# An expert loop over eight experts, with each expert's scatter in two parts and the body's last unit in two transfers

## What is computed

```python
g_idx = argmax(xt @ w_group + b_group)              # one of 4 groups of experts
top_v, top_i = lax.top_k(e_in, 2)                   # two of the 4 experts in that group
top_w = softmax(top_v) * g_w
expert = g_idx * 4 + top_i                          # 16 experts in all
y = (silu(xb @ w_gate[e]) * (xb @ w_up[e])) @ w_down[e]     # for the tokens xb of expert e
out = segment_sum(y * w, token)                     # back to the tokens, weighted
x = x + out
```

## Time and profile before

| | |
|---|---|
| median of 3 runs | 1190.21 us (1189.8 to 1192.86) |
| the profiled execution | 1189.95 us |
| its span, first to last instruction | 1188.2 us |
| mean granted TensorE clock | 0.996 of full speed |
| TensorE busy | 1133.9 us (95% of the span) |
| VectorE, ScalarE, GpSimd busy | 431.2, 174.7, 8.1 us |
| DMA | 439.30 MB, mean 370 GB/s |
| expert loops on TensorE | about 170 to 597 us, and 757 to 1184 us |

### The profile page before, as it was taken

How to read it: one execution, slowest core, us unless ns; L and a number is a source line. 1 busy time by engine, 2 the same in 40 slices (tenths; PEclk the granted TensorE clock), 3 DMA queues, 4 the chain that set the end, 5 groups by cost and what they waited for, 6 DMA issues and landing times.

```text
span 1188.2 us, 13852 instructions
## 1 busy us (share of the span) xinstructions
PE 1133.9 (95%) x5646; PEld 524.0 (44%) x5646; DVE 431.2 (36%) x766; ACT 174.7 (15%) x344; POOL 8.1 (1%) x36
## 2 busy tenths in 40 slices
PE   6998999999999999999889999999999999999997
PEld 5985443333333333333379764433333333333332
DVE  4655144232222332232276671532222323322222
ACT  3426110000000000000054261100000100000000
POOL 2000000000000000000000000000000000000000
PEclk9999999999999999999989999999999999999999
DMA  9677269999999999999994373899999999999996
GB/s 359 167 306 320 105 245 429 429 426 429 427 429 428 429 427 429 427 430 427 416 367 185 143 285 140 350 429 426 429 428 427 429 427 430 426 430 426 430 426 266
DMA packets 53904, 439.30 MB, mean 370 GB/s; under 512 B 14192, under 2 KB 14192, under 8 KB 29296
## 3 DMA queue, kind: packets, MB, share of 16 engines
q1 hardware_dynamic: 53872, 438.85, 89.1%
HBM read 437.79 MB, written 1.05 MB: 369 GB/s over the span
## 4 chain that ended last, share of the span: by engine, by line
PE 85%; DMA 9%; DVE 3%; ACT 2%; issue 1%; SPq 1%; another core or an unknown queue 0%; ACTq 0%; DVEq 0%
PE bank L1561 49%; PE bank L1471 8%; PE bank L1498 5%; PE bank L1573 5%; PE bank L1540 4%; DMA ring<-in_moe_w_gate 4%; DMA ring<-in_moe_w_up 4%; PE bank L1464 4%; PE bank L1605 1%; PE bank L1549 1%; PE bank L1355 1%; PE bank L1266 1%; PE bank L1412 1%; PE bank L1598 1%; PE bank L1306 1%
## 5 line engine op out<-in xcount | busy, mean ns | idle before, releaser
L1561 PE MATMUL bank<-ring,work 128*64 128x512 f32 x2304 | 510.8, 594 | 11.1 <-DVE work L1237 6.3
L1561 PEld LDWEIGHTS bank<-ring,work 128*64 128x64 f32 x2304 | 161.6, 137 | 343.3 <-issue 327.0
L1227 DVE TENSOR_SCALAR work<-work 128x512 f32<-128x512 f32 x32 | 13.7, 427 | 456.2 <-ACT work L786 456.2
L1229 DVE RECIPROCAL work<-work 128x512 f32<-128x512 f32 x32 | 107.3, 3353 | 1.1
L789 ACT ACTIVATE attention<-bank 128x512 f32<-128x512 f32 x32 | 19.1, 597 | 531.2 <-PE bank L1561 531.2
L1540 PE MATMUL bank<-x_sb,root_y 128*64 128x512 f32 x272 | 64.2, 593 | 2.2 <-DVE root_y L1115 2.2
L1234 DVE TENSOR_TENSOR work<-bank,work 128x512 f32<-128x512 f32 x32 | 22.1, 692 | 113.0 <-PE bank L1561 113.0
L1561 PE MATMUL bank<-ring_over_qk,work 128*64 128x512 f32 x256 | 57.7, 593 | 2.5 <-DMA ring_over_qk<-in_moe_w_gate 2.5
L1561 PE MATMUL bank<-ring_over_v,work 128*64 128x512 f32 x256 | 57.6, 592 | 0.0
L1561 PE MATMUL bank<-ring_spare,work 128*64 128x512 f32 x256 | 57.6, 592 | 0.0
L1498 PE MATMUL bank<-ring,hn 128*128 128x512 f32 x128 | 55.7, 593 | 1.2 <-ACT hn L705 0.7
(11 more groups left out here) (227 smaller groups left out, 939.6 us busy)
## 6 DMA issues: line engine op xcount, KB each, us to landing
ring<-in_moe_w_gate SPq DMA_DIRECT2D x48, 2048.0 KB, 26.9
ring<-in_moe_w_up SPq DMA_DIRECT2D x48, 2048.0 KB, 29.0
ring<-in_moe_w_down SPq DMA_DIRECT2D x48, 2048.0 KB, 27.6
ring_over_qk<-in_moe_w_gate SPq DMA_DIRECT2D x16, 2048.0 KB, 30.2
ring_over_v<-in_moe_w_up SPq DMA_DIRECT2D x16, 2048.0 KB, 30.0
ring_spare<-in_moe_w_down SPq DMA_DIRECT2D x16, 2048.0 KB, 30.7
ring<-in_ab_w_in SPq DMA_DIRECT2D x12, 1024.0 KB, 14.1
ring<-in_c_w_in SPq DMA_DIRECT2D x12, 1024.0 KB, 14.5
```

What stands on the lines that cost most here:

```text
L1229: nc.vector.reciprocal(sig, sig).then_inc(s.gate_step, 1)
L1561: last = mm(b[SLOTS * half:SLOTS * (half + 1), :], left(h, k), expert_rhs(slot, k, half), start=(h == 0 and k == 0), stop=(h == 1 and k == ...
```

## The change

Three things change, all in the expert loop.

First, a body is eight experts (an octet) instead of four: it runs twice in each layer in place of four times, and SyncE runs one pass and has one written out. Second, the scatter of the expert in front is done in two parts: its first two products (the first 128 tokens) stand between the two up units, the other two where all four stood. Third, the last unit of each body, in slot 11, is loaded by two transfers of 1024 KB; the second has a semaphore of its own, `last_rows`, and TensorE waits for it in the middle of that unit.

```diff
-QUAD = 4
-LAPS = (12, 12)
+OCTET = 8
+LAPS = (12, 12, 12, 12)
...
+SPLIT_SLOT, SPLIT_USE = PLACES[-1]
...
-            def load_unit(layer, slot, u, e):
+            def load_unit(layer, slot, u, e, split_unit=False):
                 w = (moe_w_gate, moe_w_up, moe_w_down)[u // 2][layer]
                 src = w[bass.ds(e, 1)].rearrange("e (h p s) n -> (e h) p (s n)", h=2, s=SUB)[u % 2]
+                if split_unit:
+                    sp.dma_start(ring[slot][:, 0:UNIT // 2], src[:, 0:UNIT // 2]
+                                 ).then_inc(layers[layer].unit_loaded[slot], 16)
+                    sp.dma_start(ring[slot][:, UNIT // 2:], src[:, UNIT // 2:]
+                                 ).then_inc(layers[layer].last_rows, 16)
+                    return
                 sp.dma_start(ring[slot][:, :], src).then_inc(layers[layer].unit_loaded[slot], 16)
...
-                    load_unit(layer, slot, i % UNITS, N_EXPERTS - QUAD + i // UNITS)
+                    load_unit(layer, slot, i % UNITS, N_EXPERTS - OCTET + i // UNITS,
+                              i == OCTET_UNITS - 1)
...
+                def one_half(b, left, octet, turn, h, u):
+
+                    slot, lap = place(turn, u)
+                    pe.wait_ge(s.unit_loaded[slot], octet * (USES[slot] * 16)
+                               + ((WIN if slot < UNITS else 0) + 16 * (lap + 1)))
+                    for k in range(SUB):
+                        if (turn, u) == (OCTET - 1, UNITS - 1) and k == SUB // 2:
+                            pe.wait_ge(s.last_rows, octet * 16 + 16)
+                        for half in range(2):
+                            last = mm(b[SLOTS * half:SLOTS * (half + 1), :], left(h, k),
+                                      expert_rhs(slot, k, half), start=(h == 0 and k == 0),
+                                      stop=(h == 1 and k == SUB - 1))
+                    last.then_inc(s.unit_used[slot], 1)
...
-                def scatter(count, k):
+                def scatter(count, k, tiles):
 
                     pe.wait_ge(s.giveT_ready, count)
                     pe.wait_ge(s.y_out, count)
-                    for t in range(NT):
+                    for t in tiles:
...
-                        two_halves(UP, tokens, quad, k, (2, 3))
+                        one_half(UP, tokens, octet, k, 0, 2)
+                        if k >= 1:
+                            scatter(turns(octet, k), k - 1, (0,))
+                        one_half(UP, tokens, octet, k, 1, 3)
...
                         if k >= 1:
-                            scatter(turns(quad, k), k - 1)
+                            scatter(turns(octet, k), k - 1, (1,))
...
-                    scatter(turns(quad, QUAD), QUAD - 1)
+                    scatter(turns(octet, OCTET), OCTET - 1, range(NT))
```

More of the change, by code:

```diff
@@ L142, in __init__ @@
         self.unit_loaded = [sem(f"unit_loaded{u}") for u in range(RING + 1)]
+        self.last_rows = sem("last_rows")
         self.unit_used = [sem(f"unit_used{u}") for u in range(RING + 1)]
@@ L514, in _ @@
                 sp.wait_ge(slots_ready, layer + 1)
[L515 to L522, removed]
+                last_octet = sp.value_load(last_octets[0:1, layer:layer + 1],
+                                          min_val=N_EXPERTS // OCTET - 1,
+                                          max_val=ROUNDS * N_EXPERTS // OCTET - 1)
+                with sp.Fori(0, last_octet) as octet:
+                    first = (octet & (N_EXPERTS // OCTET - 1)) * OCTET
+                    next_first = ((octet + 1) & (N_EXPERTS // OCTET - 1)) * OCTET
+                    for i in [*range(RING + 1, OCTET_UNITS), *range(RING + 1)]:
                         slot, lap = PLACES[i]
@@ L778, in _ @@
                 act.wait_ge(slots_ready, layer + 1)
[L779 to L785, removed]
+                last_octet = act.value_load(last_octets[0:1, layer:layer + 1],
+                                          min_val=N_EXPERTS // OCTET - 1,
+                                          max_val=ROUNDS * N_EXPERTS // OCTET - 1)
+                with act.Fori(0, last_octet + 1) as octet:
+                    for k in range(OCTET):
+                        now, after = turns(octet, k + 1), turns(octet, k + 2)
+                        act.wait_ge(*used(s, octet, k, 1))
                         act.activation(sig, GATE[:, :], ACT.Exp, scale=-1.0).then_inc(s.gate_exp, 1)
                         leave_gathered(after)
-                        act.wait_ge(*used(s, quad, k, 5))
+                        act.wait_ge(*used(s, octet, k, 5))
                         act.activation(y, Y[:, :], ACT.Copy).then_inc(s.y_out, 1)
                 for q in (2, 3):
-                    act.wait_ge(s.scattered, scattered_all(last_quad, q))
+                    act.wait_ge(s.scattered, scattered_all(last_octet, q))
                     if layer + 1 == LAYERS:
@@ L1218, in _ @@
                 dve.wait_ge(slots_ready, layer + 1)
[L1219 to L1226, removed]
+                last_octet = dve.value_load(last_octets[0:1, layer:layer + 1],
+                                          min_val=N_EXPERTS // OCTET - 1,
+                                          max_val=ROUNDS * N_EXPERTS // OCTET - 1)
@@ L1227, in _ @@
+                with dve.Fori(0, last_octet + 1) as octet:
+                    for k in range(OCTET):
+                        make_take(layer, turns(octet, k + 1))
+                        dve.wait_ge(s.gate_exp, turns(octet, k + 1))
                         ts(sig, sig, 1.0, None, ALU.add).then_inc(s.gate_step, 1)
-                        dve.wait_ge(s.gate_step, quad * (2 * QUAD) + (2 * k + 1))
+                        dve.wait_ge(s.gate_step, octet * (2 * OCTET) + (2 * k + 1))
                         nc.vector.reciprocal(sig, sig).then_inc(s.gate_step, 1)
-                        dve.wait_ge(s.gate_step, quad * (2 * QUAD) + (2 * k + 2))
+                        dve.wait_ge(s.gate_step, octet * (2 * OCTET) + (2 * k + 2))
```

80 lines of the change are left out of this document (37 added, 43 removed).

## The result

The changed kernel takes 1199.01 us (median of 6 runs, 1197.32 to 1200.53) against 1190.38 us for the kernel before (6 runs beside it). The ratio is 1.0066, with a 95% interval of 1.0055 to 1.0078. The forecast was 1189.1 us in a range up to 1194.0: the kernel is slower, and beyond the range.

A forecast was written before the change was run, and what follows sets the result against it. It took the DMA weight stream to bound the loops, up to each layer's last second up unit, plus a fixed TensorE chain. 2 x (-0.86 + 0.3) = -1.1 us from 1190.2 gave 1189.1 us, range 1187.0 to 1194.0.

The forecast's parts named there:

- the sum, 2 x (-0.86 + 0.3): Over two layers, 0.86 us gained behind the landing less 0.3 us for instruction packets: -1.1 us.
- the landing still decides: At each layer's last expert, the second up unit's weight transfer, not TensorE, sets the loop's end; 1.7 us of reserve remain.
- 1.7 us of reserve: TensorE's remaining slack at the last expert's second up unit: 3.4 us less 1.22 for the half scatter and 0.5 lateness.
- the 0.86 us gained: Per layer, TensorE's chain behind the last landing shortens by 1.92 - 1.06 us, as half the scatter moves ahead.
- The jump back stalls: Rival, chance 0.25: TensorE waits once per layer after the eighth expert to refetch instructions, up to 4.3 us; up to 1195.5.
- the rival's own formula: For a stall of 4.3 us at the jump back: 2 x (4.3 - 1.7 - 0.86 + 0.3) = +4.1 us.
- The packets: Four more instruction packets per layer while weights stream, from the longer body, delay the DMA by 0.3 us a layer.
- the half scatter: Between the last expert's two up units, half a scatter costs TensorE 0.86 + 0.2 = 1.06 us.
- the period of 26.3 us: TensorE's time per expert, 26.0 us before; periods above 26.3 us would show the dearer change of group.
- the price of 0.34 us for a split: In every other expert with a scatter, splitting adds two changes of group on TensorE, 2 x 0.17 us.
- dearer change of group: Rival, chance 0.05: a change between TensorE matmul shapes costs 0.5 us, a split 1.0; +12 us, 1202.
- It keeps those 0.4 us: At the last down unit, two transfers save some 0.4 us of the 0.86 otherwise lost waiting for its landing.

The follow-up runs named there:

- e1_hint: The changed kernel with the loop's jump back announced by a hint, on TensorE alone: 1191.74 us, ratio 1.0004 to the kernel before.
- e2: The changed kernel with scatter and last unit whole again, so only the bodies of eight experts remain: 1195.33 us, ratio 1.0040 to the kernel before.
- e4: The changed kernel with all 16 experts of a layer written out, no loop on any engine, both splits kept: 1192.09 us, ratio 1.0013.
- e6: The changed kernel with bodies of four experts, scatter split only in the body's last expert, last unit in one transfer: 1189.43 us, ratio 0.9991.
- e5: The changed kernel with bodies of four experts, scatter split only in the body's last expert, last unit in two transfers: 1189.26 us, ratio 0.9992.
- e7: The changed kernel with TensorE's loop starting on a boundary of the blocks in which instructions are fetched: 1199.21 us, ratio 1.0076.

## Why the forecast was wrong, step by step

**The step that failed** is the jump back: the sum, 2 x (-0.86 + 0.3), has no term for it, so it was put at nothing, and "the landing still decides" rested on that. The only row behind it was the free jump of a body half as long. The runs show 7.40 and 6.86 us a layer in its place, more than the 1.7 us of reserve and the 0.86 us gained, so TensorE's path decides and not the landing. The cause stood among the rivals, as "The jump back stalls": its place and its signs were right (a gap with no releaser after the eighth expert, 48 packets where more than 30 were named, up units without a DMA wait), but it was held for one case in four, and its price was capped at 4.3 us, so the range ended at 1194.0. That cap was the landing of a 2 KB transfer, the nearest row but of another thing. The standstill measured 4.46 and 5.17 us, and a part was missing altogether: after standing still TensorE runs at half its clock, which adds 9.95 - 7.09 = 2.86 us in layer 0 and 8.71 - 7.09 = 1.62 us in layer 1. With the measured prices, 7.40 and 6.86 us, the rival's own formula without its packets gives 2 x (7.1 - 1.7 - 0.86) = +9.1 us; +9.4 was measured. That "the body of 976 instructions seems kept" was right; that one of 1952 jumps back free too was a guess without a row.

**The reserve** of 1.7 us was close: 7.40 - 0.86 - 5.12 = 1.42 us in layer 0, 6.86 - 0.86 - 4.35 = 1.65 us in layer 1.

**The packets** were mis-sized. On record were four more per layer and 0.3 us, 0.075 us each; there were 13 more (17 against 4), since the body is fetched again in the second pass, and 11 to 13 went with 1.4 to 1.8 us, 0.12 to 0.14 us each. Where nothing was fetched again (e1_hint, layer 1) there were three more, close to the four on record. In the changed kernel this is hidden, since TensorE is later still; in e1 (layer 0), e2 and e4 it decides. Were the stall not there, the change would gain nothing: e1 loses 0.93 us in layer 0 and gains 0.95 in layer 1.

**Right** were the half scatter (1.06 us, 6.26 us behind the second up unit), the period of 26.3 us, hence the price of 0.34 us for a split, and that the "dearer change of group" does not happen. **The gain of 0.86 us** per layer arrives where the landing decides and few packets are fetched: 0.95 (e1, layer 1), 0.66 and 0.99 us (e6). In e5 it is 0.48 and 0.60. **"It keeps those 0.4 us"**, of the last unit in two transfers, was wrong: the gain is under 0.1 us.

**Not settled**: why the clock stays low longer in layer 0 than in layer 1 (changed kernel), while e7 has it the other way round; and by what rule the body of seven stalls and is fetched again, when with the hint the longer body of eight was kept in layer 1.

## What to carry to other kernels

Before a loop body is made longer, count its instructions per engine: on TensorE a body of 1464 recorded instructions jumped back free, one of 1708 stood still for 4.4 us and then ran at half clock for a while. For a body of eight experts (1952) the hint for the jump took all of that away. Code that has to be fetched is also traffic: while weights streamed at full rate here, each packet of 16 KB of instructions went with some 0.13 us of delay. And an edit that costs a little in every expert and earns once per layer (0.34 us against 0.86 us here) belongs only in the body's last expert, where it earns; here the loops became shorter by 0.5 to 1.0 us a layer, which the medians do not tell from no change.

## What was not expected of the hardware

- The standstill of TensorE cost more than itself. After 4.46 us without work its clock was granted at 0.50 from the restart at 386.52 until past 392, and 32 records took 9.95 instead of 7.09 us.
- The hint for the jump removed the whole standstill in both layers. In layer 0 the body was fetched again all the same (16 packets up to the last gate units, as against 7 in layer 1), but TensorE did not wait for it.
- Sixteen instruction packets are 0.3% of the DMA engines' time in a loop of 401 us, 1.2 us, and the weights came 1.7 us late. Why that is more than the share was not tested.
- Between six and seven experts the jump goes from free to its full standstill, with no case in between: seven already stand still for 4.38 us, eight for 4.40 (e2_octet_only). These are single runs.
